# Stick-breaking attention with the softplus in two rounded parts and all block sums as matrix products

## The reference

```python
z = jnp.einsum('bhqd,bhkd->bhqk', qb, kb) * scale
past = s_idx < t_idx
log_beta = jax.nn.log_sigmoid(z)
log_1m_beta = jnp.where(past, jax.nn.log_sigmoid(-z), 0.0)
between = lax.cumsum(log_1m_beta, axis=3, reverse=True) - log_1m_beta
weights = jnp.where(past, jnp.exp(log_beta + between), 0.0)
outs.append(jnp.einsum('bhqk,bhkd->bhqd', weights.astype(vb.dtype), vb))
```

## Time and profile before

| | |
|---|---|
| runs | 2628.25, 2624.31, 2627.62 us; median 2627.62 |
| profiled execution | 2625.41 us, span of its instructions 2623.6 us |
| TensorE busy | 2481.1 us, 95% of the span, mean granted clock 0.977 |
| VectorE busy | 1237.8 us, 47% |
| ScalarE busy | 808.9 us, 31% |
| GpSimd busy | 306.6 us, 12% |

### The profile page before, as it was taken

How to read it: one execution, slowest core, us unless ns; L and a number is a source line. 1 busy time by engine, 2 the same in 40 slices (tenths; PEclk the granted TensorE clock), 3 DMA queues, 4 the chain that set the end, 5 groups by cost and what they waited for, 6 DMA issues and landing times.

```text
span 2623.6 us, 31864 instructions
## 1 busy us (share of the span) xinstructions
PE 2481.1 (95%) x12551; PEld 2007.2 (77%) x12551; DVE 1237.8 (47%) x1580; ACT 808.9 (31%) x847; POOL 306.6 (12%) x209
## 2 busy tenths in 40 slices
PE   7499899999999989999989889999999999999999
PEld 6487688887797667887868757888787877788887
DVE  8735533335435573333553455444434435544433
ACT  5322422222315532222242363222222322322222
POOL 6402100004000040000222013000022001100000
PEclk8799999999999999999999989999999999999999
DMA  2332222233220013222332102332232221233232
GB/s 53 86 95 82 80 96 96 81 88 103 82 95 17 13 53 97 95 96 82 88 106 81 65 17 80 96 96 91 77 100 86 83 78 32 80 96 96 81 88 87
DMA packets 253601, 209.44 MB, mean 80 GB/s; under 512 B 7076, under 2 KB 251578, under 8 KB 253466
## 3 DMA queue, kind: packets, MB, share of 16 engines
q1 hardware_dynamic: 249770, 206.02, 25.6%
q0 software_dynamic: 720, 1.51, 0.2%
q10 hardware_dynamic: 3040, 0.92, 0.2%
HBM read 203.97 MB, written 2.10 MB: 79 GB/s over the span
## 4 chain that ended last, share of the span: by engine, by line
PE 87%; DVE 6%; issue 2%; ACT 2%; POOL 1%; SPq 1%; ACTq 0%; DMA 0%; DVEq 0%; POOLq 0%
PE psum L799 15%; PE psum L801 15%; PE psum L800 15%; PE psum L832 9%; PE psum L833 8%; PE psum L834 8%; PE psum L917 2%; PE psum L918 2%; PE psum L919 2%; POOL tmp_a L529 1%; PE psum L953 1%; PE psum L971 1%; SPq L403 1%; DVE tmp_b L1986 1%; PE psum L947 1%
## 5 line engine op out<-in xcount | busy, mean ns | idle before, releaser
L1360 ACT CAST w_hi<-w_stage 128x2048 fp32r<-128x2048 f32 x209 | 399.3, 1911 | 1390.4 <-PE psum L801 744.4
L1955 DVE TENSOR_TENSOR w_lo<-w_stage,w_hi 128x2048 fp32r<-128x2048 f32 x202 | 475.7, 2355 | 694.8 <-ACT w_hi L1360 694.7
L832 PE MATMUL psum<-x_hi,w_hi 128*128 128x512 f32 x944 | 380.3, 403 | 41.5 <-DVE x_lo L2090 16.5
L833 PE MATMUL psum<-x_lo,w_hi 128*128 128x512 f32 x944 | 372.2, 394 | 0.0
L834 PE MATMUL psum<-x_hi,w_lo 128*128 128x512 f32 x944 | 371.5, 393 | 0.0
L800 PE MATMUL psum<-x_lo,w_hi 128*128 128x512 f32 x944 | 367.2, 389 | 0.0
L799 PE MATMUL psum<-x_hi,w_hi 128*128 128x512 f32 x944 | 367.2, 389 | 0.0
L801 PE MATMUL psum<-x_hi,w_lo 128*128 128x512 f32 x944 | 367.2, 389 | 0.0
L799 PE MATMUL psum<-hidden_hi,w_hi 128*128 128x512 f32 x768 | 300.5, 391 | 8.0 <-DVE w_lo L1955 2.9
L800 PE MATMUL psum<-hidden_lo,w_hi 128*128 128x512 f32 x768 | 298.9, 389 | 0.0
L801 PE MATMUL psum<-hidden_hi,w_lo 128*128 128x512 f32 x768 | 298.8, 389 | 0.0
(11 more groups left out here) (398 smaller groups left out, 3003.1 us busy)
## 6 DMA issues: line engine op xcount, KB each, us to landing
w_stage<-in_ffn_w_gu_dram SPq DMA_DIRECT2D x44, 1024.0 KB, 5.0
w_stage<-in_ffn_w_down_dram SPq DMA_DIRECT2D x64, 704.0 KB, 4.5
w_stage<-in_ffn_w_gate_dram SPq DMA_DIRECT2D x22, 1024.0 KB, 5.3
w_stage<-in_ffn_w_up_dram SPq DMA_DIRECT2D x22, 1024.0 KB, 5.3
w_stage<-in_sb_w_qkv_dram SPq DMA_DIRECT2D x12, 1024.0 KB, 5.2
w_stage<-in_od_w_in_dram SPq DMA_DIRECT2D x12, 1024.0 KB, 5.3
w_stage<-in_ev_w_in_dram SPq DMA_DIRECT2D x10, 1024.0 KB, 5.2
w_stage<-in_ssm_w_glu_dram SPq DMA_DIRECT2D x8, 1024.0 KB, 5.6
```

The source lines that it names most:

```text
L832: nc.tensor.matmul(dst[u], hi, x_hi, start=(k == order[0]), stop=False)
L833: nc.tensor.matmul(dst[u], hi, x_lo, start=False, stop=False)
L1360: nc.scalar.copy(whi[:, half, :], wst[:, half, :]).then_inc(whi_done, 1)
L1955: V.tensor_tensor(wlo[:, half, :], wst[:, half, :], whi[:, half, :].bitcast(F32), ALU.subtract).then_inc(wlo_done, 1)
```

## The change

Three things are changed.

1. The softplus of a head is split into two rounded parts. GpSimd, which did nothing in this stage, rounds it (`sp_hi`), part 0 and then part 1; VectorE subtracts (`sp_lo`). Both are kept for two heads. The sums run as rounded products, one with `sp_hi` and one with `sp_lo`, and take the two negated masks in rounded form. VectorE makes these masks at the start of the v stage; before, GpSimd did.
2. The block sums `drop_sum` are gone. Each later block has its product with `neg_ones` instead.
3. The values lie at the start of the hidden buffers, the attention output goes to `x_hi` and `x_lo` instead of the hidden buffers, and the residual stays in its own buffer, so `out_stage` no longer rebuilds it.

```diff
-        v_t = at("v_tok", [P, TT, D], res_at)
+        v_t = at("v_tok", [P, TT, D], hid_at)
...
-        drop_sum = at("drop_sums", [P, 2, 3 * P], hid_at + 81 * KB)
-        neg_up_to = at("neg_up_to", [P, P], hid_at + 84 * KB)
-        neg_ones = at("neg_ones", [P, P], hid_at + 84 * KB + 512)
+        sp_hi = [at(f"sp_hi{n}", [P, STICK], hid_at + (42, 52)[n] * KB, F32R) for n in range(2)]
+        sp_lo = [at(f"sp_lo{n}", [P, STICK], hid_at + (47, 81)[n] * KB, F32R) for n in range(2)]
+        neg_up_to = at("neg_up_to", [P, P], hid_at + 86 * KB, F32R)
+        neg_ones = at("neg_ones", [P, P], hid_at + 86 * KB + 512, F32R)
...
             deviation_sums(1)
 
-            pool.wait_ge(consts, 4)
-            pool.wait_ge(x_ready, 2 * DC + 1)
-            nc.gpsimd.memset(neg_ones[:, :], -1.0).then_inc(neg_ready, 1)
-            nc.gpsimd.tensor_scalar(neg_up_to[:, :], up_to[:, :], -1.0, 0.0, ALU.mult, ALU.add).then_inc(neg_ready, 1)
+            for h in range(HEADS):
+                for part in range(2):
+                    cols = STICK_PARTS[part]
+                    pool.wait_ge(sp_done, 2 * h + part + 1)
+                    if h >= 2:
+                        pool.wait_ge(cs_done, 2 * (h - 2) + part + 1)
+                    nc.gpsimd.tensor_copy(sp_hi[h % 2][:, cols], stick[h % 6][:, cols]).then_inc(hi_done, 1)
...
             def stick_sums(h):
 
                 flat = psum[:, 4 * (h % 2):4 * (h % 2) + 3, :].rearrange("p b n -> p (b n)")
-                sp = stick[h % 6]
-                pe.wait_ge(sp_done, 2 * h + 1)
-                nc.tensor.matmul(flat[:, 0:SEQ], neg_up_to[:, :], sp[:, 0:SEQ], start=False, stop=True, skip_group_check=True)
-
-                pe.wait_ge(sp_done, 2 * h + 2)
+                both = (sp_hi[h % 2], sp_lo[h % 2])
+
+                def add(weight, to, frm, n):
+                    for sp in both:
+                        mm = nc.tensor.matmul(flat[:, to:to + n], weight, sp[:, frm:frm + n], start=False, stop=True,
+                                              skip_group_check=True)
+                    return mm
+
+                pe.wait_ge(lo_done, 2 * h + 1)
+                add(neg_up_to[:, :], 0, 0, SEQ).then_inc(cs_done, 1)
                 for j in range(TT - 1):
-                    mm = nc.tensor.matmul(flat[:, REST[j]:REST[j] + P], neg_ones[:, :], sp[:, (j + 1) * P:(j + 2) * P],
-                                          start=False, stop=True, skip_group_check=True)
-                mm.then_inc(cs_done, 1)
-                for c0, c1 in ((512, 1024), (1024, STICK)):
-                    nc.tensor.matmul(flat[:, c0:c1], neg_up_to[:, :], sp[:, c0:c1], start=False, stop=True,
-                                     skip_group_check=True)
-                pe.wait_ge(sums_done, 3 * h + 3)
-                for to, c0, c1 in ((REST[1] + P, 2 * P, 3 * P), (REST[0] + P, 0, 2 * P)):
-                    mm = nc.tensor.matmul(flat[:, to:to + c1 - c0], neg_ones[:, :], drop_sum[:, h % 2, c0:c1], start=False,
-                                          stop=True, skip_group_check=True)
-                mm.then_inc(cs_done, 1)
+                    add(neg_ones[:, :], REST[j], (j + 1) * P, SEQ - (j + 1) * P)
+                pe.wait_ge(lo_done, 2 * h + 2)
+                add(neg_ones[:, :], REST[0] + P, REST[1], 2 * P)
+                add(neg_ones[:, :], REST[0] + 2 * P, REST[2], P)
+                add(neg_ones[:, :], REST[1] + P, REST[2], P)
+                add(neg_up_to[:, :], 512, 512, 512)
+                add(neg_up_to[:, :], 1024, 1024, STICK - 1024).then_inc(cs_done, 1)
...
             def stick_weights(h, part):
 
                 act.wait_ge(cs_done, 2 * h + part + 1)
-                act.wait_ge(sums_done, 3 * h + 3)
...
             def out_stage(name, n):
                 st = ST[name]
-                if 0 < n < 4:
-
-                    for c in range(DC):
-                        link(V.tensor_tensor(res[:, c, :], xhi[:, c, :].bitcast(F32), xlo[:, c, :].bitcast(F32), ALU.add))
...
-                dve.wait_ge(sp_done, 2 * h + 2)
-                if h >= 2:
-                    dve.wait_ge(cs_done, 2 * (h - 2) + 2)
-                total = drop_sum[:, h % 2, :]
-                V.tensor_tensor(total[:, 2 * P:3 * P], sp[:, REST[2]:REST[2] + P], sp[:, 3 * P:4 * P], ALU.add).then_inc(sums_done, 1)
-                V.tensor_tensor(total[:, 0:P], sp[:, REST[1]:REST[1] + P], sp[:, 2 * P:3 * P], ALU.add).then_inc(sums_done, 1)
-
-                dve.wait_ge(sums_done, 3 * h + 1)
-                V.tensor_tensor(total[:, P:2 * P], sp[:, REST[1] + P:REST[1] + 2 * P], total[:, 2 * P:3 * P],
-                                ALU.add).then_inc(sums_done, 1)
+                for part in range(2):
+                    cols = STICK_PARTS[part]
+                    dve.wait_ge(hi_done, 2 * h + part + 1)
+                    if h >= 2:
+                        dve.wait_ge(cs_done, 2 * (h - 2) + part + 1)
+                    V.tensor_tensor(sp_lo[h % 2][:, cols], sp[:, cols], sp_hi[h % 2][:, cols].bitcast(F32),
+                                    ALU.subtract).then_inc(lo_done, 1)
...
             def v_stage():
 
                 st = ST["v"]
+                dve.wait_ge(consts, 3)
+                V.tensor_scalar(neg_up_to[:, :], up_to[:, :], -1.0, 0.0, ALU.mult, ALU.add).then_inc(neg_ready, 1)
+                V.tensor_scalar(neg_ones[:, :], ones[:, :], -1.0, 0.0, ALU.mult, ALU.add).then_inc(neg_ready, 1)
```

More of the change, by code:

```diff
@@ L314, in build_blocks @@
             sem(n) for n in "shift_done ln_shifted dev_sq ln_m2 ln_var".split())
-        neg_ready, z_done, abs_done, exp_done, ln_part, sp_done, sums_done = (
-            sem(n) for n in "neg_ready z_done abs_done exp_done ln_part sp_done sums_done".split())
+        neg_ready, z_done, abs_done, exp_done, ln_part, sp_done, hi_done, lo_done = (
+            sem(n) for n in "neg_ready z_done abs_done exp_done ln_part sp_done hi_done lo_done".split())
         cs_done, w_done, o_done, o_hi, o_ready = (sem(n) for n in "cs_done w_done o_done o_hi o_ready".split())
@@ L1210, in _ @@
                 elif name == "w_o":
-                    feature_stage(name, hhi, hlo, lambda k: (o_ready, k + 2), 2, last_mix)
+                    feature_stage(name, xhi, xlo, lambda k: (o_ready, k + 2), 2, last_mix)
                     norm(2)
@@ L2146, in stick_soft @@
                                            ALU.max, ALU.add).then_inc(sp_done, 1)
-                dve.wait_ge(sp_done, 2 * h + 2)
-                if h >= 2:
-                    dve.wait_ge(cs_done, 2 * (h - 2) + 2)
-                total = drop_sum[:, h % 2, :]
-                V.tensor_tensor(total[:, 2 * P:3 * P], sp[:, REST[2]:REST[2] + P], sp[:, 3 * P:4 * P], ALU.add).then_inc(sums_done, 1)
-                V.tensor_tensor(total[:, 0:P], sp[:, REST[1]:REST[1] + P], sp[:, 2 * P:3 * P], ALU.add).then_inc(sums_done, 1)
-                dve.wait_ge(sums_done, 3 * h + 1)
-                V.tensor_tensor(total[:, P:2 * P], sp[:, REST[1] + P:REST[1] + 2 * P], total[:, 2 * P:3 * P],
-                                ALU.add).then_inc(sums_done, 1)
+                for part in range(2):
[5 more added lines that the diff above has]
+                                    ALU.subtract).then_inc(lo_done, 1)
             def put_pair(p):
                 dve.wait_ge(o_done, p + 1)
-                V.tensor_copy(hhi[:, p, :], bank[7]).then_inc(o_hi, 1)
+                V.tensor_copy(xhi[:, p, :], bank[7]).then_inc(o_hi, 1)
                 dve.wait_ge(o_hi, p + 1)
-                V.tensor_tensor(hlo[:, p, :], bank[7], hhi[:, p, :].bitcast(F32), ALU.subtract).then_inc(o_ready, 1)
+                V.tensor_tensor(xlo[:, p, :], bank[7], xhi[:, p, :].bitcast(F32), ALU.subtract).then_inc(o_ready, 1)
             def v_stage():
                 st = ST["v"]
+                dve.wait_ge(consts, 3)
+                V.tensor_scalar(neg_up_to[:, :], up_to[:, :], -1.0, 0.0, ALU.mult, ALU.add).then_inc(neg_ready, 1)
+                V.tensor_scalar(neg_ones[:, :], ones[:, :], -1.0, 0.0, ALU.mult, ALU.add).then_inc(neg_ready, 1)
                 for i in range(st.iters):
```

## The result

| | before | changed |
|---|---|---|
| median of 19 runs each, same chip | 2628.05 us (2624.24 to 2634.62) | 2635.65 us (2629.49 to 2646.21) |
| profiled execution, its span | 2625.41, 2623.6 us | 2635.65, 2633.9 us |
| mean granted clock | 0.977 | 0.971 |

The ratio is 1.003, with a 95% interval from 1.0021 to 1.004: 7.6 us more, and 5.5 to 10.5 by the interval. The change makes the kernel slower by 0.3%. 2637 had been predicted.

The account below looks back on a forecast made before the run. TensorE was taken to set the pace at 7.52 us per head, VectorE having 0.96 to spare. 10.8 for 14 heads less 0.35 at the tail gave +10.4 us, forecast 2637, range 2629 to 2644.

Parts of the forecast that it names:

- What bounds it: Stick-breaking stage before the change: TensorE sets the pace at 7.52 us per head, VectorE has 0.96 to spare.
- Behind `stick_soft` part 1: VectorE's way from there to the next head: 2.45 us in place of 0.72, making a head 7.70.
- The lock-out: GpSimd's rounding of part 1 is held off until VectorE's low part 0 ends, then needs 0.74 us more.
- The rival of no lock-out: GpSimd's rounding runs beside low part 0: a head 7.29 us, +4.3 in all, 2631; chance 0.17.
- TensorE's sums: Block sums of a head as 18 rounded products: 2.71 us (2.35 to 3.3) in place of 3.67.
- The rival of a gain: TensorE keeps the pace and gets faster: 14 heads take 92 to 98 us, kernel about 2616; chance 0.08.
- The clock: Forecast: TensorE's clock stays 1.00 in the stage. Rival: it falls, adding 10 to 15 us, 2650; chance 0.07.
- The tail: From `stick_abs` of head 15 to the first product of w_o: 10.65 us in place of 11.0, giving back 0.35.
- The residual: Dropping eight VectorE sums, 5.77 us, after the stage gains nothing, since TensorE's products of w_o hid them.
- the masks and the output pairs: Masks made on VectorE at the v stage's start and output pairs sent to `x_hi`, `x_lo`: no time either way.
- the chain term: VectorE's longer work over 14 heads of the stage: 116.1 us, 10.8 more than 105.3.
- The signs: Expected in the profile after: `stick_abs` 7.7 or 9.1 us apart, VectorE waiting about 0.8 for GpSimd, TensorE idle 1 or more per head.

Follow-up runs that it names:

- low part 0 early: Changed kernel with VectorE's subtraction of part 0 moved in front of `stick_soft` part 1: 2626.45 us, ratio 0.9999 to the kernel before.
- the interleaved kernel: On top of low part 0 early, low part 1 between the next head's `stick_abs` parts, `put_pair` between `stick_soft` part 0 and low part 0: 2619.37 us.
- the filler: Changed kernel with four unread rounded products of 512 columns behind each mix on TensorE: 2634.04 us, ratio 1.0023 to the kernel before.
- the kernel with two extra operations: Kernel before with two unread VectorE additions of 768 columns per head, behind and in front of the drop sums: 2632.22 us, ratio 1.0019.
- part 1 rounded on VectorE: The kernel with low part 0 early, part 1's rounding on VectorE instead of GpSimd: 2625.19 us, ratio 0.9993 to the kernel before.

## Why the prediction was right

**What bounds it.** Right. TensorE set the pace before, and VectorE had little to spare. The spare was 1.17, not 0.96: I had added durations and left out that operations in line overlap by 0.08 each. Since the change adds 1.57 a head (5.76 to 7.33), more than either, this didn't turn the forecast. It does decide the rival below.

**Behind `stick_soft` part 1: 2.45 predicted, 2.20 measured** (812.52 to 814.72). Its terms: low part 0 and the held rounding together 1.39 predicted, 1.29 measured (to 813.81); the handoff back from GpSimd 0.1 predicted, 0.03 measured; low part 1 0.96 predicted, 0.88 in effect, as `stick_abs` starts 0.08 before it ends. The rest of the chain was 5.13 in place of 5.25, and `put_pair` 1.33 in place of 1.38. So 7.33 a head in place of 7.70, and 14 x 7.33 + 6 x 1.33 = 110.6 in place of 116.1: the term was 5.5 too large.

**The lock-out.** Right, and the whole loss hangs on it: with low part 0 early the rounding is 0.83, the head 6.93, the kernel as fast as before. The chain is then 1.17 longer than before, just what VectorE had to spare. The rival of no lock-out was priced too high, at 7.29 a head and +4.3 us. As in the earlier trace rows, the held rounding had part of its time behind it: it ended 0.69 after low part 0's end at 813.12, not 0.83 after. `stick_abs`, which reads PSUM, doesn't hold it: in the interleaved kernel a rounding of part 1 runs beside `stick_abs` and takes its bare 0.83, in VectorE's and GpSimd's order of time:

```profile
811.94 0.68 DVE L2137 TENSOR_SCALAR stick<-psum 128x512 int32<-128x512 int32 x1
...
812.09 0.83 POOL L553 CAST sp_hi<-stick 128x768 fp32r<-128x768 f32 x1 [1.97 <-DVE stick L2148]
```

The Trainium skill (SBUF — State Buffer, Who interferes with whom) says that a VectorE instruction with at most one SBUF input, outside the modes that use both ports, doesn't contend with GpSimd. By this rule, the trace agrees.

**TensorE's sums: 2.71 predicted, 2.84 measured** (821.11 to 823.95), some 0.1 to 0.2 of it gaps between groups. The six narrow products, which no row of before had, came 0.05 to 0.12 apart: 0.57 together, where I had taken 0.72 and had set 0.64 beside it. Four of them in TensorE's order of time:

```profile
822.72 0.23 PE L969 MATMUL psum<-sp_hi,neg_ones 128*128 128x128 f32 x1
822.79 0.27 PE L969 MATMUL psum<-sp_lo,neg_ones 128*128 128x128 f32 x1
822.89 0.27 PE L969 MATMUL psum<-sp_hi,neg_ones 128*128 128x128 f32 x1
823.01 0.28 PE L969 MATMUL psum<-sp_lo,neg_ones 128*128 128x128 f32 x1
823.12 0.44 PE L969 MATMUL psum<-sp_hi,neg_up_to 128*128 128x512 f32 x1
```

**The rival of a gain** had its price right. I gave 92 to 98 us for the 14 heads and 2616 for the kernel, if VectorE's chain fell under TensorE's. The interleaved kernel is that case: 96.5 and 2619.4.

**The clock.** Here the forecast failed in part. It said that the clock stays 1.00, and gave its fall 0.07 with a price of 10 to 15 us. It fell three times within the stage, at a price of about 3 us. In the 14 heads it is 1.1: the first fall makes the head from 838.03 to 847.51 0.8 longer than its 8.66 and the next one 0.3, since the scores come late in VectorE's order of time:

```profile
839.31 0.96 DVE L2136 TENSOR_SCALAR stick<-psum 128x768 int32<-128x768 int32 x1 [0.60 <-PE psum L957]
```

The second fall changed no head's length (8.65 from 887.10 to 895.75). The other 0.3 of 111.98 - 110.6 = 1.4 lies in the first head, 7.63 here and 7.64 with the filler, so it isn't the clock's. In the last sums the ten products behind low part 1 (its end 919.15) would have been done 1.5 later at full clock, at 920.7, and were at 922.7: 2.0. The filler, which left one short fall, took 1.1 off the heads and 0.9 off the last sums. The price of 10 to 15 was too high because a fall touches a head or two and TensorE's slack covers most of it.

**The tail: -0.35 predicted, +1.55 measured** (911.74 to 924.30 is 12.56; before 11.01). By VectorE's chain alone w_o would have started at 920.7 + 1.45 = 922.2, 0.5 less than before, so the term was right at full clock; the fall took 2.0.

**The residual: nothing predicted, nothing measured** (ratio 1.0004). The same holds for the masks and the output pairs: no row of the stage shows them on the path; they weren't run by themselves.

**The sum.** Up to the shift it is +5.3 (VectorE's chain in 14 heads) + 0.3 (first head) + 1.1 (clock) + 1.55 (tail, with 2.0 of the clock) = 8.2, where +10.4 was predicted. Two errors cancel in part: the chain term 5.5 too large, the clock of 3.1 left out. So the mechanism was right, and that the total came so near is in part luck. The medians moved by 7.6, not 10.4, and 2637 lies 1.4 from the measured time also because the base of the forecast was 1.5 below the median that the kernel before then had. What the profiled execution loses behind the shift was not tested; the two profiles of the changed kernel differ there, with falls of the clock at other places.

**The signs.** Seen: VectorE's wait for GpSimd (0.72), low part 1 well behind `stick_soft` (1.32), no change by the residual. Missed: `stick_abs` came 7.33 and 8.66 apart, not 7.7 and 9.1; the rounding was 0.39 longer, not 0.5; and TensorE's idle time was 0.4 a head, not 1 or more, and ended on ScalarE's weights in the heads, on VectorE's low part only in the last sums.

## What to carry to other kernels

Before work goes to an idle engine, read how much the engine that must wait for it has to spare per round, and put the handoff where that engine waits anyway. Here the same operations in three orders on VectorE gave 2636, 2626 and 2619 us. Shortening one engine's work gains only down to the next longest chain. Find that chain's length by adding operations of known cost until the time moves.

## What the runs showed of the hardware

A GpSimd rounding of 768 columns that starts 0.15 behind a VectorE subtraction with both inputs in SBUF takes 1.22 in place of 0.83. One case in the kernel before points the other way round: the VectorE operation of the earlier trace rows took 1.10 and the one ahead of it, of the same line and shape, 0.74. A GpSimd copy from SBUF to SBUF had started 0.08 before the longer one. No run tests this by itself. In VectorE's and GpSimd's order of time:

```profile
1541.44 0.74 DVE L2322 SCALAR_TENSOR_TENSOR qn_pair<-qk_feat,params,qk_rstd 128x512 f32<-128x512 f32 x1
...
1542.02 0.64 POOL L586 COPY vb_pair<-value_tok 128x512 f32<-128x512 f32 x1 [11.28 <-PE psum L1088]
```

From GpSimd's end to VectorE's waiting instruction it is 0.03 us, from VectorE's to GpSimd's 0.07 (812.52 to 812.59).

I had not expected such short idle times to cost the clock. In the changed kernel TensorE idled at most 1.7 us at a time over 800 to 850 (46.5 of 50 us busy), and its granted clock fell from 2.4 GHz to 1.2 GHz (0.50) for up to 10 us. In the kernel with two extra operations, which also idles in each head, it stayed at 1.00 in that stretch, and so it did with part 1 rounded on VectorE. Later in the stage it fell there as well (means of 0.97 and 0.93 over 850 to 900). In the interleaved kernel, where TensorE's idle times in the heads were 0.4 at most, it didn't fall in the 14 heads. Which pattern of idle time brings the fall isn't settled by these runs.

A rounded product of 128 columns was followed by the next product after 0.05 to 0.12 us.
